# PEER gates: scattered into HBM by indirect DMAs and multiplied in by VectorE, in place of one-hot products on TensorE; a denser top-k; whole sparse rows

## The chip, the cores and the metric

The kernel runs on one core of a Trainium2 chip. The metric is the time of one execution on the device in microseconds. In this text PE is TensorE, PEld its weight loads, DVE is VectorE, ACT is ScalarE, POOL is GpSimd and SP is SyncE, as in the profile.

## What is computed

One decoder layer over 256 tokens of width 2048: a hybrid mixer, a cross attention, then the PEER expert layer, which takes two thirds of the time (571 of 1912 us lie ahead of it, with its queries) and is all that the change touches (besides sixteen stores that the front issues). For every token 8 heads pick 16 of 128 x 128 experts each:

```python
s1, i1 = lax.top_k(s[:, :, 0], 16)
s2, i2 = lax.top_k(s[:, :, 1], 16)
cand_s = s1[..., :, None] + s2[..., None, :]          # 16 x 16 sums
top_s, top_pos = lax.top_k(cand_s, 16)
experts = (i1 * 128 + i2) at top_pos
gates = softmax(top_s)
act = gelu(u[experts] @ x)                            # u, v: 16384 x 2048
y = sum over the 128 picks of gates * act * v[experts]
```

## The kernel before

*Dense and sparse tokens.* The first 224 tokens (TD) are computed densely: PE multiplies all 16384 rows of u with them, the result is multiplied by a gate that is zero for experts not picked, and PE multiplies that with all of v. The last 32 tokens (TS) are computed sparsely, by gathering the picked rows of u and v from HBM.

*Pieces and chunks.* All weights come as pieces of 128 x 1024 floats (512 KB), loaded by SP into 4 buffers (raw). ACT rounds a piece into its high part (whi, `high` and `high_v`), the rest is the low part (wlo), and PE does 16 matmuls a piece: 8 of the high part with 448 columns (inputs' high and low), 8 of the low part with 224 columns. whi and wlo have 3 buffers each, so the high part of piece n can only be made when PE has done with piece n-3. The front (mixer, cross attention, queries) has 180 pieces, the U part 256 and the V part 256. Two pieces of U are a chunk: 128 experts (one i1, all i2) for 224 tokens. Loops have 12 pieces (BODY), 6 chunks.

*Low parts.* POOL makes them for the front, all of U and the first 8 pieces of V (L438); from there on DVE makes them (`v_step`, L1437), with the low part of the gated activations (L1439).

*U.* PE leaves a chunk's sums in one of 3 PSUM banks, DVE joins their two halves (`join`, L1234), ACT applies gelu. Until chunk 48 (C_TABLES) DVE also does the top-k (L1278 to L1335): 8 pairs of lists, with a join between its parts, at fixed places of the code. The chosen i1, i2 and gates are then transposed on PE (L1925), the sparse tokens' are selected with a product (L1930). From chunk 54 (C_GATE) on, each pair of tokens gets its 128 x 128 matrix of gates: DVE writes one-hot rows of i1 and of i2 times gate (`hot_i1` L1382, `hot_i2` L1376), PE multiplies them (`gate_products`, L1899, 2 matmuls of 256 columns, 5 pairs in 6 pieces, 112 pairs), DVE adds the halves (L1405) and multiplies them into W for these tokens over all chunks (L1412). Gelus of late chunks stand in PSUM until DVE multiplies them in (`take_chunk`, L1391).

*V.* PE waits for the low part of the piece and of the gated activations (`v_ready`). Beside it, POOL issues 256 indirect gathers of 128 rows of 512 floats (four partitions share a row, 12 buffers); DVE takes each with one instruction (`u_row` L1445, `v_row` L1458). Two products (FOLD) add sums across partitions.

The order on each engine's queue is written out by hand. DVE's queue in V is: low part, low part of the gated activation, then what stands at that piece (rows, residual additions, sums of blocks). ACT's is: high part, high part of the gated activation, then its DMAs. Where an engine waits for a semaphore, all behind it in its queue waits.

## Time and profile before

| | |
|---|---|
| time, median of 3 runs | 1914.01 us (1913.36 to 1915.1) |
| span of the profiled execution | 1912.2 us |
| PE busy / PEld busy | 1896.7 us (99%) / 1758.9 us (92%) |
| DVE / ACT / POOL busy | 1383.4 us (72%) / 950.5 us (50%) / 1390.8 us (73%) |
| mean granted PE clock | 0.997 |
| HBM read and written | 443.04 MB and 4.19 MB, 234 GB/s over the span |
| front, U, V and tail (starts of their first products) | 0 to 571.3, to 1251.3, to 1899, to 1912.2 us |

In order of time:

```profile
PE   9999999999999999999999999999999999999997
DVE  7534684045545777968888888479889889999986
POOL 3867768887998999998888888976555525666711
```

A digit is the busy share of one of 40 equal slices (47.8 us), in tenths. POOL is full while it makes low parts (up to slice 26), DVE fuller in V, where it makes them.

### The profile page before, as it was taken

How to read it: one execution, taken by the hardware profiler on the slowest of the kernel's cores; microseconds unless marked ns; L12 is line 12 of the kernel's file. 1: busy time of each engine (PE TensorE's matmuls, PEld its weight loads, DVE VectorE, ACT ScalarE, POOL GpSimd, SP SyncE). 2: the span in 40 equal slices, each digit the busy share in tenths (PEclk: the TensorE clock that was granted, in tenths of full speed). 3: DMA queues.
4: the chain of work that ended last, by engine and by line, in shares of the span. 5: the costliest groups of instructions: out<-in, count | busy, mean ns of one | idle time of the engine just before them, and what ended most of it. 6: DMA issues, size and time to landing. Idle time of an engine off the chain costs nothing.

```text
span 1912.2 us, 35061 instructions
## 1 busy us (share of the span) xinstructions
PE 1896.7 (99%) x11798; PEld 1758.9 (92%) x11798; DVE 1383.4 (72%) x2585; ACT 950.5 (50%) x1342; POOL 1390.8 (73%) x708
## 2 busy tenths in 40 slices
PE   9999999999999999999999999999999999999997
PEld 7888889888999999999999999999999999999997
DVE  7534684045545777968888888479889889999986
ACT  6453355475544444544444444455555555555555
POOL 3867768887998999998888888976555525666711
PEclk9999999999999999999999999999999999999999
DMA  8544546564655666666666566689999988999984
GB/s 307 186 143 153 199 144 224 193 190 155 218 188 177 207 209 208 210 202 196 194 192 196 189 195 195 200 280 351 333 336 334 333 297 298 337 325 334 328 273 145
DMA packets 128380, 448.29 MB, mean 234 GB/s; under 512 B 16528, under 2 KB 19472, under 8 KB 127632
## 3 DMA queue, kind: packets, MB, share of 16 engines
q1 hardware_dynamic: 102240, 367.29, 58.5%
q0 software_dynamic: 20480, 67.13, 10.0%
q10 hardware_dynamic: 5584, 12.88, 2.0%
q8 instruction: 45, 0.74, 0.2%
q14 instruction: 31, 0.25, 0.0%
HBM read 443.04 MB, written 4.19 MB: 234 GB/s over the span
## 4 chain that ended last, share of the span: by engine, by line
PE 72%; POOL 17%; issue 8%; DMA 1%; DVE 1%; ACT 0%; POOLq 0%; SPq 0%; DVEq 0%; ACTq 0%
PE ps L1885 22%; PE ps L1982 22%; POOL wlo L438 17%; PE ps L1888 12%; PE ps L1985 11%; PE ps L1899 1%; PE ps L1585 1%; PE ps L1587 1%; PE ps L1586 1%; PE ps L1961 1%; DMA raw<-in_w_front 0%; PE ps L1869 0%; DMA big<-in_x_t 0%; PE ps L1963 0%; ACT whi L539 0%
## 5 line engine op out<-in xcount | busy, mean ns | idle before, releaser
L438 POOL TENSOR_TENSOR wlo<-raw,whi 128x1024 fp32r<-128x1024 f32 x436 | 1057.6, 2430 | 207.9 <-ACT whi L539 193.1
L539 ACT ACTIVATE whi<-raw 128x1024 fp32r<-128x1024 f32 x435 | 461.2, 1060 | 633.7 <-PE ps L1888 361.8
L1885 PE MATMUL ps<-x_parts,whi 128*128 128x448 f32 x2048 | 588.9, 369 | 0.0
L1982 PE MATMUL ps<-gate_parts,whi 128*128 128x448 f32 x1992 | 573.6, 369 | 0.0
L734 ACT ACTIVATE whi<-raw 128x1024 fp32r<-128x1024 f32 x256 | 271.7, 1061 | 294.9 <-PE ps L1985 255.8
L1888 PEld LDWEIGHTS ps<-x_parts,wlo 128*128 128x128 f32 x2048 | 384.7, 188 | 31.3
L1985 PEld LDWEIGHTS ps<-gate_parts,wlo 128*128 128x128 f32 x1992 | 374.2, 188 | 30.8
L1888 PE MATMUL ps<-x_parts,wlo 128*128 128x224 f32 x2048 | 386.9, 270 | 0.0
L1985 PE MATMUL ps<-gate_parts,wlo 128*128 128x224 f32 x1992 | 376.0, 270 | 0.0
L1437 DVE TENSOR_TENSOR wlo<-raw,whi 128x1024 fp32r<-128x1024 f32 x248 | 303.9, 1225 | 68.1 <-ACT whi L734 52.1
L1885 PEld LDWEIGHTS ps<-x_parts,whi 128*128 128x128 f32 x2048 | 310.3, 191 | 0.0
L1982 PEld LDWEIGHTS ps<-gate_parts,whi 128*128 128x128 f32 x1992 | 301.2, 191 | 0.1
L1585 PE MATMUL ps<-whi,x_parts 128*128 128x512 f32 (+1 forms) x544 | 214.1, 394 | 2.3 <-DVE wlo L888 2.3
L1587 PE MATMUL ps<-whi,x_parts 128*128 128x512 f32 (+1 forms) x544 | 210.1, 386 | 0.0
L1586 PE MATMUL ps<-wlo,x_parts 128*128 128x512 f32 (+1 forms) x544 | 209.4, 385 | 0.0
L465 POOL DMA_INDIRECT gather_low<-in_w_v,big x88 | 115.9, 1317 | 110.7 <-DVE big L1458 80.3
L465 POOL DMA_INDIRECT gather_low<-in_u_rows,big x88 | 103.9, 1180 | 67.3 <-DVE big L1445 54.3
L1234 DVE TENSOR_REDUCE big<-ps 128x224 f32<-128x448 f32 x128 | 79.4, 620 | 88.2 <-PE ps L1888 87.7
L1585 PEld LDWEIGHTS ps<-whi,x_parts 128*128 128x128 f32 x544 | 102.5, 188 | 23.8 <-DVE x_parts L868 3.5
L1587 PEld LDWEIGHTS ps<-whi,x_parts 128*128 128x128 f32 x544 | 102.6, 189 | 21.7
L1586 PEld LDWEIGHTS ps<-wlo,x_parts 128*128 128x128 f32 x544 | 102.7, 189 | 20.2
L1439 DVE TENSOR_TENSOR gate_parts<-big,gate_parts 128x224 fp32r<-128x224 f32 x256 | 112.7, 441 | 1.1 <-ACT gate_parts L737 0.6
(266 smaller groups left out, 2217.2 us busy)
## 6 DMA issues: line engine op xcount, KB each, us to landing
raw<-in_w_u SPq DMA_DIRECT2D x256, 512.0 KB
raw<-in_w_v SPq DMA_DIRECT2D x256, 512.0 KB
raw<-in_w_front SPq DMA_DIRECT2D x180, 512.0 KB
big<-in_mem ACTq DMA_DIRECT2D x8, 256.0 KB, 5.6
big<-in_mem_t ACTq DMA_DIRECT2D x2, 1024.0 KB, 6.2
big<-in_x ACTq DMA_DIRECT2D x2, 1024.0 KB, 7.3
x_back<-x2t_scratch ACTq DMA_DIRECT2D x2, 896.0 KB
big<-in_x_t SPq DMA_DIRECT2D x3, 512.0 KB, 8.4
```

The costliest lines, as they stand in the source:

```text
L438: nc.gpsimd.tensor_tensor(wlo[:, j % SPL, :], raw[:, j % RAW, :], whi[:, j % SPL, :], ALU.subtract).then_inc(lo_done, 1)
L465: nc.gpsimd.indirect_dma_start(ROW[at_row], None, table, bass.IndirectOffsetOnAxis(index.bitcast(I32), 0)).then_inc(row_in[at_row], 16)
L539: nc.scalar.activation(whi[:, j % SPL, :], raw[:, j % RAW, :], ACT.Copy).then_inc(hi_done, 1)
L734: nc.scalar.activation(whi[:, (V0 + j) % SPL, :], raw[:, j % RAW, :], ACT.Copy).then_inc(hi_done, 1)
L1437: nc.vector.tensor_tensor(wlo[:, s, :], raw[:, j % RAW, :], whi[:, s, :], ALU.subtract).then_inc(lo_v_done, 1)
L1585: nc.tensor.matmul(out_ap, sh, mh, start=start, stop=False)
L1586: nc.tensor.matmul(out_ap, sh, ml, start=False, stop=False)
L1587: return nc.tensor.matmul(out_ap, sl, mh, start=False, stop=stop)
L1885: nc.tensor.matmul(sums[:, 0:2 * TD], whi[:, s, cols], x_parts[:, :, m, 0:TD], start=m == 0, stop=False, skip_group_check=True)
L1888: ins = nc.tensor.matmul(sums[:, TD:2 * TD], wlo[:, s, cols], xh[:, m, 0:TD], start=False, stop=m == DC - 1, skip_group_check=True)
L1982: nc.tensor.matmul(sums[:, 0:2 * TD], whi[:, s, cols], gate_parts[:, g, :, 0:TD], start=False, stop=False, skip_group_check=True)
L1985: ins = nc.tensor.matmul(sums[:, TD:2 * TD], wlo[:, s, cols], gate_parts[:, g, 0, 0:TD], start=False, stop=False, skip_group_check=True)
```

## The change

1. *Gates by scatter.* While the front runs, ACT issues 16 stores of zeros (`zero_gates`, 896 KB each) that clear an array of 128 x 128 x 224 floats in HBM. After the top-k DVE computes one cell number for each pick and token; POOL issues 256 indirect DMAs (8 heads, 2 blocks of 128 and 96 tokens, 16 picks), each adding one gate per token into its cell. A head's DMAs wait for those of the head before, block by block. Then POOL loads the gates back, 4 chunks at a time (`load_gates`, 448 KB, 2 buffers, 32 loads), and DVE multiplies them into W (`scale_by_gate`, 128 x 896 columns): 24 of them beside chunks 112 to 126 of U, 8 at every second piece of V from piece 2.
2. *PE loses* the one-hot products, the transposes, the fold and the norm product. The selection for the sparse tokens is 16 small products instead of 4.
3. *Low parts.* POOL makes those of the front and of the first 72 pieces of U, but for the piece at place 10 of each 12, which DVE makes after the join of a chunk. All the rest of U and V is DVE's.
4. *Denser top-k.* It must end by chunk 36 (C_TABLES), not 48. A join is put in whenever the reckoned work since the last has reached 4.2 us (`topk_work`). The second list's values lie in PSUM.
5. *Whole sparse rows.* A partition takes a whole row of 2048 floats: 32 gathers of u and 32 of v, of 128 rows of 8 KB (1 MB), 3 buffers, in place of 128 and 128 of 256 KB. The four groups of partitions are added at the end by copies through DMAs issued by ACT and four additions on DVE (pieces 240, 241, 242 and 251).
6. PE waits for the join of a chunk, no longer for its gelu, to reuse the bank.

```diff
+C_TABLES = 36
+PER_LOAD = 4
+SCALED_FROM, SCALED_IN_U = 112, 24
+RING = 3
+ADDED_AT = (*range(240, 239 + GROUPS), 251)
+U_VECTOR = 10
+TOPK_NS = 4200
...
+            with pool.Fori(U0 // BODY, U0 // BODY + E_BODIES) as i:
+                for j in range(BODY):
+                    if j != U_VECTOR:
+                        rest_of(i * BODY, j)
+
+            pool.wait_ge(zeros_out, 16 * NK // (2 * PER_LOAD))
+            pool.wait_ge(cells_ready, 1)
+            for head in range(PH):
+                for tb in range(TB):
+                    if head:
+                        pool.wait_ge(scattered[tb], 16 * TOPK * head)
+                    tokens = min(P, PITCH - tb * P)
+                    for k in range(TOPK * head, TOPK * (head + 1)):
+                        nc.gpsimd.indirect_dma_start(gates_d, bass.IndirectOffsetOnAxis(CELLS[0:tokens, tb, k:k + 1].bitcast(I32), 0),
+                                                     TOP_GATES[0:tokens, tb, k:k + 1], None,
+                                                     compute_op=ALU.add).then_inc(scattered[tb], 16)
+            for tb in range(TB):
+                pool.wait_ge(scattered[tb], 16 * TOPK * PH)
+            def load_gates(k):
+                if k >= 2:
+                    pool.wait_ge(scaled_by_gate, k - 1)
+                pool.dma_start(gates_of[:, k % 2].rearrange("p a b -> p (a b)"),
...
+            for k in range(SCALED_IN_U + 2):
+                load_gates(k)
+            pool.wait_ge(picks, 1)
+            for n in range(RING):
+                gather(n)
+            for k in range(SCALED_IN_U + 2, LOADS):
+                load_gates(k)
+            for n in range(RING, 2 * PER):
+                gather(n)
...
             for j in range(BODY):
                 high_v(LAST_BODY * BODY, j)
                 gated_high(LAST_BODY * BODY - NK, j)
+                if j == 3:
+                    for k in range(2, GROUPS):
+                        act.wait_ge(group_added, k - 1)
+                        load_addend(k)
+                    act.wait_ge(group_added, GROUPS - 1)
+                    act.dma_start(ADDEND[GROUPS], gain_rows[1].partition_broadcast(TS)).then_inc(last_gain_s_in, 16)
...
             def join(k0, c):
+                nc.vector.reduce_sum(W[:, k0 + c, :], sums, AX).then_inc(sums_joined, 1)
+                if not isinstance(k0, int) or C_TABLES - 2 <= k0 + c < NK - 2:
+                    low_u(k0 * 2, 2 * c + 4)
+                    low_u(k0 * 2, 2 * c + 5)
+                elif k0 + c < C_TABLES and c % CHUNKS_PER_BODY == U_VECTOR // 2 - 2:
+                    low_u(k0 * 2, 2 * c + 4)
+            def topk_work(ns):
+                spent[0] += ns
+                if spent[0] >= TOPK_NS:
+                    spent[0] -= TOPK_NS
+                    join(0, next(chunk))
...
+            def scale_by_gate(k):
+                dve.wait_ge(act_taken, PER_LOAD * (k + 1))
+                dve.wait_ge(gates_in[k % 2], 16 * (k // 2 + 1))
+                some = W[:, PER_LOAD * k:PER_LOAD * (k + 1), :]
+                nc.vector.tensor_tensor(some, some, gates_of[:, k % 2, :, 0:TD], ALU.mult).then_inc(scaled_by_gate, 1)
+            def add_group(k):
+                dve.wait_ge(group_in[k], 16)
+                if k:
+                    dve.wait_ge(group_added, k)
+                nc.vector.tensor_tensor(Y_S, Y_S, ADDEND[k], ALU.add).then_inc(group_added, 1)
...
+                v_step(j)
+                if j % 2 == 0 and scaled < LOADS:
+                    scale_by_gate(scaled)
+                    scaled += 1
...
+                while done < 2 * PER and j >= taken(done):
+                    row_taken(done)
+                    done += 1
+                if j in ADDED_AT:
+                    add_group(ADDED_AT.index(j))
...
-                pe.wait_ge(lo_done, i * BODY + (U0 + j + 1))
+                pe.wait_ge(*low_of_u(i, j, late))
...
-            def gate_products(i, j):
-                for m in range(2):
-                    ins = nc.tensor.matmul(ps[:, 4 + j % 2, m * 2 * P:(m + 1) * 2 * P], hot1_row[:, m, :],
-                                           hot2_rows[:, j % 2, m].rearrange("p a b -> p (a b)"), start=True, stop=True)
-                ins.then_inc(gate_mat, 1)
```

## Rows read from the trace of the kernel before

**Rows 1.** Table of stretches; the second line names the columns, x counts instructions

```profile
core 0: us, PE busy (x) PEld busy (x) DVE busy (x) ACT busy (x) POOL busy (x), PEclk, DMA share, GB/s
650.00:700.00 50.00, 50.00 (x320) 47.56 (x319) 36.80 (x129) 23.66 (x31) 47.90 (x21) 1.00 0.65 207
...
1300.00:1400.00 100.00, 100.00 (x637) 95.12 (x636) 89.01 (x176) 53.00 (x80) 59.84 (x50) 1.00 0.96 338
```

**Rows 2.** Timeline of PE in U: start, length, instruction; sixteen rounds apart

```profile
699.83 0.38 PE L1888 MATMUL ps<-x_parts,wlo 128*128 128x224 f32 x2
...
709.91 0.38 PE L1888 MATMUL ps<-x_parts,wlo 128*128 128x224 f32 x2
```

**Rows 3.** Timeline of PE: first U product, transposes and selection, first V product

```profile
571.30 0.58 PE L1885 MATMUL ps<-x_parts,whi 128*128 128x448 f32 x2
...
820.37 0.81 PE L1925 MATMUL ps<-big 128*128 128x128 f32 x6
...
821.84 0.65 PE L1885 MATMUL ps<-x_parts,whi 128*128 128x448 f32 x2
...
1251.25 0.37 PE L1961 MATMUL ps<-gate_parts,whi 128*128 128x448 f32 x1
```

**Rows 4.** The gate products: count, shortest/median/longest ns, first and last start

```profile
L1899 PE MATMUL ps<-hot_rows,hot_row x224: 280/282/285, 854.7 to 1215.9; 128*128 128x256 f32 x112
```

**Rows 5.** DVE's groups in U: shapes, count, busy us, mean ns, idle before

```profile
L1234 DVE TENSOR_REDUCE big<-ps 128x224 f32<-128x448 f32 x52 | 32.2, 620 | 54.3 <-PE ps L1888 53.8
L1289 DVE TENSOR_TENSOR big<-big 128x256 f32<-128x256 f32 x16 | 26.5, 1696 | 0.0
...
L1330 DVE TENSOR_REDUCE big<-ps 128x128 f32<-128x2048 f32 x4 | 9.1, 2280 | 0.0
...
L1412 DVE TENSOR_TENSOR big<-ps,big 128x256 f32 x100 | 42.7, 427 | 15.5 <-DVE ps L1405 7.8 <-DVE big L1391 0.5
```

**Rows 6.** Timeline of DVE behind the last list: first and last of three

```profile
766.57 2.63 DVE L1315 CAST big<-big 128x512 f32<-128x512 uint32 x1
...
771.53 2.49 DVE L1317 TENSOR_SCALAR big<-big 128x256 uint32<-128x256 uint32 x1
```

**Rows 7.** Low parts on POOL and on DVE: shortest/median/longest ns, first and last start

```profile
L438 POOL TENSOR_TENSOR wlo<-raw,whi x436: 2342/2403/3395, 26.8 to 1266.0; 128x1024 fp32r<-128x1024 f32 x146
...
L1437 DVE TENSOR_TENSOR wlo<-raw,whi x248: 1211/1226/1262, 1268.7 to 1892.4; 128x1024 fp32r<-128x1024 f32 x124
```

**Rows 8.** The gathers: two groups of four, and one in the timeline of POOL

```profile
L465 POOL DMA_INDIRECT gather_low<-in_u_rows,big x88: 940/1142/1847, 1268.7 to 1524.7; - x88
...
L465 POOL DMA_INDIRECT x_back<-in_w_v,big x40: 944/1076/2652, 1552.9 to 1812.1; - x40
...
1272.69 0.95 POOL L465 DMA_INDIRECT gather_low<-in_u_rows,big  x1 [0.30 <-issue]
```

**Rows 9.** DMA issues: queue, count, KB each, median us from issue to landing

```profile
big<-in_sub_keys ACTq DMA_DIRECT2D x1, 1024.0 KB, 4.8
...
x2t_scratch<-big ACTq DMA_DIRECT2D x1, 448.0 KB, 2.9
...
x_scratch<-big ACTq DMA_DIRECT2D x1, 256.0 KB, 3.1
```

**Rows 10.** DMA rate in 40 slices of 1266 to 1300 us

```profile
GB/s 236 106 304 222 135 364 306 205 222 325 357 328 333 376 395 405 395 390 405 395 405 405 400 410 390 400 400 333 410 357 251 414 386 357 395 270 414 366 318 381
```

**Rows 11.** Timeline of ACT at the start of V

```profile
1261.70 1.74 ACTq L764 DMA_DIRECT2D big<-in_gain_rows  x4
...
1276.05 1.06 ACT L734 ACTIVATE whi<-raw 128x1024 fp32r<-128x1024 f32 x1 [2.95 <-remote]
```

**Rows 12.** DVE's row operations in V, 512 columns

```profile
L1445 DVE CUSTOM_DVE_ANT_0 gather_low<-gather_low,big 128x512 f32<-128x512 f32 x88 | 59.3, 686 | 0.0
```

**Rows 13.** Timeline of DVE at the end: scaling of the sparse rows, last joins

```profile
1895.95 0.75 DVE L1540 SCALAR_TENSOR_TENSOR big<-big,stats 128x512 f32<-128x512 f32 x1
1896.62 4.34 DVE L1471 TENSOR_REDUCE big<-ps 128x224 f32<-128x448 f32 x8
```

653 lines of the change are left out of this document (280 added, 373 removed).

## The prediction

> **What bounds the kernel now.** I read the table of stretches first [rows 1]: in each stretch of the expert part TensorE (PE) is busy for all of it, and its granted clock is 1.00, the 2.4 GHz level. Busy isn't yet bound, so I took the timeline of PE: sixteen rounds of 0.63 us lie between 699.83 and 709.91, four pieces of 2.52 us [rows 2], the same in the V part (637 matmuls, 39.8 pieces, in 100 us [rows 1]). GpSimd's low part takes 2.40 us of each 2.52 (47.90 of 50 us busy [rows 1], [rows 7]) and never makes PE wait here. So the U and V parts are 2 x 256 pieces x 2.52 = 1290 us in which PE is the bound; only what leaves PE's queue, or makes PE wait, moves the end. The front (571 us) is untouched but for sixteen DMA issues on ScalarE at about 0.45 us each (four take 1.74 [rows 11]), against 1.9 us of slack a piece; I cost them at nothing, 0 to 2 us.
>
> **Removed from PE.** The 224 gate products start between 854.7 and 1215.9 [rows 4]. By the code, 133 pieces and 111 pairs lie between the first pair and the last, so a pair costs (361.2 - 133 x 2.52) / 111 = 0.235 us, and 112 pairs cost 26.3 us. The whole of U agrees: 1251.25 - 571.30 = 679.95 us [rows 3], less 256 x 2.52 = 645.1, less two key products (7.2), the transposes and selections (1.47, from 820.37 to 821.84 [rows 3]) leaves 26.2. The fold and norm products give back 0.3. The selection becomes 16 small products, some 0.15 us each by that same stretch, 2.4 instead of 1.47: +0.9. PE's sum alone: 1914.0 - 26.3 - 0.3 + 0.9 = 1888.3. The profiled span is 1912.2, 1.8 below the median; I apply all differences to the median.
>
> **New waits.** Call S(n) the time when PE starts piece n and T(c) the end of chunk c (two pieces). ScalarE can make the high part of piece n only after S(n-2), and it is ready at S(n-2)+1.1; the low part is due at S(n), 5.04 later. VectorE (DVE) needs 1.23 us for it [rows 7], so DVE may be 2.6 us late before PE stops. That slack is the measure for everything below.
>
> (a) *Denser top-k.* Before, a pair of lists has four joins, 20.2 us, at 36.80 of 50 us busy [rows 1]: 14.8 us, less four joins of 0.62 and two additions of 1.70 [rows 5] is 8.9 us. With one operand in PSUM the addition should cost 0.43, as L1412 does [rows 5], so 9.8 us a pair. The change gives a pair 2.76 joins, 13.9 us of PE, against 9.8 + 1.7: it fits. The additions run from 0.77 to 2.63 us beside GpSimd, 1.70 on average. The Trainium skill, "SBUF — State Buffer", section "Who interferes with whom", says that a VectorE instruction with two SBUF inputs contends with a GpSimd one that reads SBUF; by it moving one operand to PSUM ends the wait, else the pair costs 12.3 + 1.7, still about 13.9.
> The end of top-k doesn't fit. By the code's counter join 25 comes right before the three casts and shifts, which take 7.5 us [rows 6] where they stand now and the counter reckons 2.0. Then one cast to PSUM and three operations of 2.3 us on 2048 columns: join 27 starts at T(25) + 0.5 + 0.8 + 7.5 + 0.7 + 3 x 2.3 + 0.5 = 16.9 ([rows 5, 6]; 0.5 is a join, 0.8 a copy and a subtraction), not +10.1. Its chunk is one of those whose join is followed by DVE's only low part of the body (piece 58), due at T(25)+15.1 and done at 18.6, or 19.8 if it waits for a GpSimd operation of 2.4 us. PE stops 3.5 to 4.7 us; I take 4.7. The same happens at piece 70 behind the gates and cells, 0 to 3.4 us, depending on whether each short operation waits for a 2.4 us one; I take 1. Sum +5.7 (0 to 9).
>
> (b) *Late U.* DVE does a join (0.62) and two low parts (2.45) a chunk of 5.04 us; the second must await ScalarE and ends at T+4.9. Due at T+7.6: nothing, 0 to 1. Cover: if it goes, each us costs a us.
>
> (c) *The scatters.* 256 DMAs on GpSimd's queue, from about T(33) to the first scale at chunk 112: some 158 pieces, 398 us, 1.55 us each. No row shows a scatter, let alone an adding one. The nearest is the indirect gather of as many rows: 0.94 us at the shortest and 1.85 at the longest in the u rows (2.65 in v's), median 1.14, plus 0.30 between two [rows 8]; a period of 1.24 to 2.15, mean 1.48. In V, DVE's two-input operations fill 64% of the time, in late U 49%, so I take 1.45: 371 us, 27 us early. Bounds 317 and 550 us. The 16 waits for the head before lie 16 DMAs (23 us) behind their DMA: nothing.
> What the trace can't give is the time that a DMA engine needs for a 4-byte element; no row has one. The Trainium skill, "DMA: Bandwidth & Descriptors", section "Specifications", says that transfers below 512 B make the DMA engine read, modify and write; no run here shows it, and it speaks against this change.
>
> (d) *Scaling in U.* 24 scales of 4 x 224 columns, at DVE's rate 1.09 us each, in 15 chunks: 0.62 + 2.45 + 1.75 = 4.8 of 5.04 us. Their gates come 448 KB at a time in two buffers, and a load is issued only when its buffer is scaled. 448 KB took 2.9 us and 1 MB 4.8 us to land [rows 9]; with 1.24 us for GpSimd's issue [rows 8] and 1.09 for a scale a pair takes 5.2 to 7.1 us where 6.3 are there. Taken: 1.5, bounds 0 and 12.
>
> (e) *Start of V.* GpSimd issues three whole-row gathers of 1 MB when U ends, and behind them, in the same queue, the load for scale 26. DVE wants scale 26 at piece 6, and PE waits unless it lands by 15 us into V. Until then weights need 208 GB/s (512 KB per 2.52 us), the queue must move 3.6 MB, and ScalarE's queue 1 MB of x rows and then 1 MB of gain. The stretch where V starts now shows 400 to 410 GB/s at the top [rows 10], and ScalarE already waited 2.95 us there [rows 11]. 3.6 MB at 200 GB/s is 18 us, with 1 MB beside it 23, plus 2.5 before they start less what a stopped PE frees: 19 to 24 us. Taken +8, bounds 0 and 12.
>
> (f) *Rows in V.* A row operation of 512 columns costs 0.69 [rows 12], nearly all by length; 2048 columns 2.3, one every 3.2 pieces: late by 1.4 us (2.3 + 1.6 - 2.52), under 2.6. The bytes and their rate stay (338 GB/s [rows 1]). Taken 0.5 (0 to 5).
>
> (g) *End.* DVE's third group sum stands at piece 242, but ScalarE issues its load after the high part of 243, at S(241)+1.8. With 3.1 us to land [rows 9], 2.3 for the sum and 1.6 for the two low parts piece 243 is ready at S(241)+8.8, due at +5.04: +3.8 (2 to 5). Sum and square at 251 and 252: +0.7. Behind the last piece the scaling of the sparse rows, 0.75 now, stands ahead of the joins, which PE's last products await [rows 13]: 2.3 instead, +1.5.
>
> **Sum.** 1888.3 + 5.7 + 1.5 + 8 + 0.5 + 3.8 + 0.7 + 1.5 = 1910, of which the waits are 21.7. I forecast 1909, as the casts' waits are taken near their top.
>
> **Rivals.**
> *No wait bites.* If DVE's lateness is absorbed and the loads land early, PE's sum holds, with the tail: 1890. For it: PE never stopped in U though DVE ran late at the same casts (joins had three banks then, no low part). Against it: orders written in the code (e, g) that no faster engine mends. 0.22.
> *The scatters come late.* Decides at 1.55 us a scatter, against 1.45 expected. Each 0.1 us above it holds DVE at chunk 112, and PE behind it, for 25.6 us; at 1.65 the time is 1935, at 2.15 it is 1909 + 152 = 2061. Slower than before. For it: the slow gathers reach past it, and adding is unpriced. Against: the mean, and only 96 tokens in every second one. 0.22.
> *The scatters' packets crowd out the weights.* The 16 DMA engines are 0.65 busy in U [rows 1], which leaves 0.5 us per scatter and engine for its 8 elements; above 60 ns an element, weights land late and PE slows in some 370 us: at 100 ns the engines would need 1.2 times their time, +74 us, 1983. 0.06. The skill's rule on transfers below 512 B would do this; its time is the one just given.
> *Gates don't leave PE's path,* because DVE is the bound in U instead: late U needs 3.1 of 5.04 us, so I give it none of its own.
>
> **Numbers.** Forecast 0.50. A difference within 0.2%, 3.8 us, is about what can't be told from no change, so faster ends at 1910.2 and slower starts at 1917.8. The forecast's own range of 1899 to 1920 splits into 0.27 faster, 0.21 same and 0.02 slower. With the first rival (0.22 faster) and the other two (0.28 slower): 0.49, 0.21, 0.30. The range takes in the first rival and a scatter of up to 1.65 us: 1889 to 1936, leaving out most of the long waits.
>
> **What would show it.** No rows of the gate products, and pieces of 2.52 us still. PE idle before its pieces 58 and 70 (about 4.7 and 1 us) released by DVE's low part; a gap of some 8 us at piece 7 of V with DVE waiting for the gate load; 4 us at piece 243 behind the addition of a group. The last scatter ends about 25 us before the first scale. Wrong if DVE's wait before its first scale is long (scatters), if ScalarE waits for weight loads in late U (packets), or if PE has no gaps (1890).

## The result, and the profile after

The changed kernel takes 2106.8 us (2106.7 to 2108.6, 4 runs), the kernel before 1914.6 us on the same chip (1913.4 to 1915.6, 4 runs): a ratio of 1.1006 with a 95% interval of 1.0991 to 1.1022, slower by 192 us. The forecast was 1909 us, with a range of 1889 to 1936: wrong in sign and in size. The profiled execution has a span of 2104.8 us.

The page's first two parts show where the time went: four slices of 53 us in which TensorE (PE), VectorE (DVE) and ScalarE (ACT) stand for all or most of the time, while GpSimd (POOL) is at 8 tenths in three of them.

```profile
span 2104.8 us, 32557 instructions
...
PE   9999999999999999999999200488999999999997
...
DVE  7543780256368976666666000476888888888877
ACT  7443364655444444444444000143555554555554
POOL 4767688778978788888888888411121120211201
PEclk9999999999999999999999655698999999999998
```

The waits of PE and DVE (engine, line, what was waited for: us in total, times, the longest):

```profile
PE ps L1903 <- DVE wlo L1296: 183.7, 6, 176.8
PE ps L1969 <- DVE gate_parts L1460: 10.0, 4, 5.8
PE ps L1951 <- DVE gate_parts L1460: 5.0, 2, 4.9
...
DVE big L1445 <- DMA gates_of<-gates_scratch: 196.2, 14, 178.1
```

And the groups (busy us, mean ns, idle before by releaser):

```profile
L512 POOL DMA_INDIRECT gates_scratch<-big x256 | 492.7, 1925 | 81.5 <-issue 81.5
...
L1445 DVE TENSOR_TENSOR big<-big,gates_of 128x896 f32<-128x896 f32 x32 | 34.9, 1089 | 196.3 <-DMA gates_of<-gates_scratch 196.2
```

They read as one chain. DVE waits 178.1 us for the first load of gates, at its first scale; PE waits 176.8 us for the low part queued behind that scale. The load stands behind 256 scatters of 1.925 us with 0.318 us between two, a period of 2.24 us and 574 us in all, from 762 to 1336 us. That mean is of two kinds: 161 scatters with a period of 2.5 us up to 1165 us, and 95 with one of 1.8 us after it, while PE and DVE stand. It is the prediction's rival "the scatters come late", which I gave 0.22, beyond the 2.15 us that it prices. It names 1.55 us as the point from which it decides.

### The profile page after: what moved, and what is told of

Same layout as the page of the kernel before. It is cut to its first block, busy times and chain, and to the rows that moved or that the text cites. A ratio compares the mean times of both kernels' runs of the same rounds, so it can differ in the third digit from the quotient of the medians.

```text
span 2104.8 us, 32557 instructions
## 1 busy us (share of the span) xinstructions
PE 1890.3 (90%) x11586; PEld 1746.5 (83%) x11586; DVE 1326.9 (63%) x1882; ACT 952.2 (45%) x1342; POOL 1209.1 (57%) x607
## 4 chain that ended last, share of the span: by engine, by line
POOL 46%; PE 31%; issue 14%; DMA 4%; DVE 3%; ACT 0%; POOLq 0%; DVEq 0%; ACTq 0%; SPq 0%
POOL gates_scratch L512 23%; POOL wlo L475 23%; PE ps L1969 18%; PE ps L1972 10%; DMA gates_of<-gates_scratch 2%; DMA raw<-in_w_v 1%; DVE big L1445 1%; PE ps L1603 1%; PE ps L1604 1%; PE ps L1605 1%; DVE wlo L1458 1%; PE ps L1951 1%; DVE wlo L1296 1%; ACT whi L787 0%; POOLq L474 0%
## 5 line engine op out<-in xcount | busy, mean ns | idle before, releaser
L475 POOL TENSOR_TENSOR wlo<-raw,whi 128x1024 fp32r<-128x1024 f32 x238 | 580.6, 2447 | 176.3 <-ACT whi L588 170.8
L1969 PE MATMUL ps<-gate_parts,whi 128*128 128x448 f32 x2000 | 580.3, 372 | 10.1 <-DVE gate_parts L1460 10.0
L512 POOL DMA_INDIRECT gates_scratch<-big x256 | 492.7, 1925 | 81.5 <-issue 81.5
L1458 DVE TENSOR_TENSOR wlo<-raw,whi 128x1024 fp32r<-128x1024 f32 x256 | 313.0, 1223 | 99.8 <-ACT whi L787 98.7
L1296 DVE TENSOR_TENSOR wlo<-raw,whi 128x1024 fp32r<-128x1024 f32 x190 | 231.7, 1225 | 137.7 <-ACT whi L588 137.7
L1445 DVE TENSOR_TENSOR big<-big,gates_of 128x896 f32<-128x896 f32 x32 | 34.9, 1089 | 196.3 <-DMA gates_of<-gates_scratch 196.2
L746 ACT ACTIVATE big<-big (+1 forms) x128 | 48.2, 376 | 196.7 <-DVE big L1303 196.5
L532 POOL DMA_INDIRECT gather_low<-in_v_rows,big x21 | 35.5, 1689 | 166.9 <-DVE big L1473 120.7
L1603 PEld LDWEIGHTS ps<-whi,x_parts 128*128 128x128 f32 x544 | 102.6, 189 | 23.9 <-DVE x_parts L933 3.4
```

Of the source, the lines that this page charges most:

```text
L475: nc.gpsimd.tensor_tensor(wlo[:, j % SPL, :], raw[:, j % RAW, :], whi[:, j % SPL, :], ALU.subtract).then_inc(lo_done, 1)
L512: nc.gpsimd.indirect_dma_start(gates_d, bass.IndirectOffsetOnAxis(CELLS[0:tokens, tb, k:k + 1].bitcast(I32), 0), TOP_GATES[0:tokens, tb, k ...
L1296: nc.vector.tensor_tensor(wlo[:, (U0 + n) % SPL, :], raw[:, n % RAW, :], whi[:, (U0 + n) % SPL, :], ALU.subtract).then_inc(lo_u_done, 1)
L1458: nc.vector.tensor_tensor(wlo[:, s, :], raw[:, j % RAW, :], whi[:, s, :], ALU.subtract).then_inc(lo_v_done, 1)
L1603: nc.tensor.matmul(out_ap, sh, mh, start=start, stop=False)
L1969: nc.tensor.matmul(sums[:, 0:2 * TD], whi[:, s, cols], gate_parts[:, g, :, 0:TD], start=False, stop=False, skip_group_check=True)
```

## Why a scatter takes 2.24 us

GpSimd's timeline beside DVE's low parts, and where DVE stands (start, length, instruction, idle time before it):

```profile
771.66 1.53 POOL L512 DMA_INDIRECT gates_scratch<-big  x1 [0.30 <-issue]
773.50 1.53 POOL L512 DMA_INDIRECT gates_scratch<-big  x1 [0.30 <-issue]
...
787.59 2.22 POOL L512 DMA_INDIRECT gates_scratch<-big  x1 [0.30 <-issue]
790.11 2.21 POOL L512 DMA_INDIRECT gates_scratch<-big  x1 [0.30 <-issue]
...
1177.41 1.54 POOL L512 DMA_INDIRECT gates_scratch<-big  x1 [0.30 <-issue]
1179.25 1.54 POOL L512 DMA_INDIRECT gates_scratch<-big  x1 [0.30 <-issue]
```

DVE's timeline in the middle of these:

```profile
787.16 1.23 DVE L1296 TENSOR_TENSOR wlo<-raw,whi 128x1024 fp32r<-128x1024 f32 x1 [0.35 <-ACT whi L588]
789.68 1.23 DVE L1296 TENSOR_TENSOR wlo<-raw,whi 128x1024 fp32r<-128x1024 f32 x1 [1.29 <-ACT whi L588]
```

From 769.8 to 774.5 us, where DVE has no low part, and from 1170 us on, where it stands, a scatter of 128 tokens takes 1.53 us (one of 96 takes 1.43). Beside low parts it takes 2.2, and the starts are 2.52 us apart: one scatter a piece of U. My theory from these rows: the instruction by itself is dear (1.5, not the gather's 0.94 of [rows 8]), and DVE's operation with two SBUF inputs adds 0.7. The rivals were room for descriptors, the addition's own traffic in HBM, and waits that would be there with fewer scatters too.

**Half the scatters.** The four first heads only; the gates of the others are left out.

```diff
-            for head in range(PH):
+            for head in range(PH // 2):
...
-                pool.wait_ge(scattered[tb], 16 * TOPK * PH)
+                pool.wait_ge(scattered[tb], 16 * TOPK * PH // 2)
```

> The changed kernel with 128 of its 256 scattering DMAs: only heads 0 to 3 are scattered, so the gates of heads 4 to 7 are left out of the dense tokens. Everything else, the 56 gate products included, is as in the changed kernel. Theory A (the count of scatters times their period of 2.24 us passes the 388 us that lie between the start at 762 us and the first scale at chunk 112): the last scatter is issued near 762 + 128 x 2.24 = 1049 us, 100 us before VectorE wants gates, the wait of 176.8 us at the last chunks of U goes whole, with about 2 us at the lower clock behind it, and the time is 2106.8 - 177 - 2 = about 1928 us. What then remains above the 1888 us of the sum is small: the gaps of 3.9 us (top-k), 4.9 and 7.1 (start of V), 2.5 (end) and the rest. Rival B (the scales in U are late by themselves, for the load of their gates or VectorE's work, and the scatters only add to it): a wait of tens of us stays before chunk 112 to 127, and the time is above 1950 us. Rival C (the scatters' packets in HBM are what costs, and half of them slows the weights as well): TensorE shows gaps at the casts in the stretch from 762 to 1049 us.

Measured: 1927.8 us (1925.6 to 1929.4, 4 runs), 1.0067 [1.0050, 1.0084] of before. The long wait is gone, 179 us with it, as the count demands. The scatters took 2.20 us each, with a period of 2.51. (The gate products that the expectation names are in neither kernel.) But 1928 is 40 us above PE's sum of 1888; that is the next section's matter.

**No addition in the DMA.** Of a cell that several heads pick, one gate stays and the others are left out.

```diff
-                                                     TOP_GATES[0:tokens, tb, k:k + 1], None,
-                                                     compute_op=ALU.add).then_inc(scattered[tb], 16)
+                                                     TOP_GATES[0:tokens, tb, k:k + 1], None).then_inc(scattered[tb], 16)
```

> The changed kernel with its 256 scatters writing plainly, without the addition in the DMA: of cells that several heads pick, one gate is kept and the others are left out. Theory A (a scatter's time is GpSimd's own work on its instruction and what VectorE's two-input operations beside it add): the scatters stay at 2.1 to 2.3 us beside VectorE's low parts and 1.5 us where VectorE stands, or fall both by the same amount if the addition is part of the dear instruction; with 1.14 us as for a gather of 2 KB rows the period would be 1.14 + 0.30 = 1.44 without VectorE and about 2.1 beside it. Rival B (the read and write back of the 4-byte addition in HBM fills the queue, and GpSimd waits for room in it): the time from issue to landing falls from 4.9 us to about 3, the scatters fall to about 1.2 us everywhere, the last ends near 762 + 256 x 1.5 = 1146 us, and the time falls by over 150 us, to about 1940 us.

> The kernel with plain scatters (the addition of several heads' gates in one cell is left out) once more, since its first time rests on one execution and kernels near it fall into slow issue of TensorE: 1926 to 1930 us in each execution if it is free of that, or over 2000 in some of them if it is a matter of chance from execution to execution.

Measured: 1928.0 us, and 1928.2 (1925.6 to 1931.6, 4 runs) the second time. GpSimd's timeline of the first, beside DVE's unchanged low part:

```profile
789.33 0.98 POOL L512 DMA_INDIRECT gates_scratch<-big  x1 [0.30 <-issue]
790.62 0.91 POOL L512 DMA_INDIRECT gates_scratch<-big  x1 [0.31 <-issue]
791.83 1.06 POOL L512 DMA_INDIRECT gates_scratch<-big  x1 [0.30 <-issue]
```

And DVE's in the same stretch:

```profile
790.88 1.23 DVE L1295 TENSOR_TENSOR wlo<-raw,whi 128x1024 fp32r<-128x1024 f32 x1 [0.41 <-ACT whi L587]
```

All 256 take 0.968 us in the mean, a period of 1.27, and end at 1088 us. So without the addition both terms are gone: 0.55 us of the instruction and nearly all of what the low parts added. I had taken the two for separate; the second hangs on the first. Of the two forecasts rival B's (1.2 us, last end at 1146 us, about 1940 us) came nearer than mine, so this run alone doesn't say whether GpSimd's own work or the traffic is the cost; the next two runs bear on that. The number of packets changes too. The DMA queue of GpSimd in 800 to 1080 us, in the changed kernel (112 scatters in that stretch) and then without the addition (223 scatters):

```profile
q0 software_dynamic: 14000, 0.06, 9.2%
```

```profile
q0 software_dynamic: 7137, 0.11, 1.8%
```

The columns are packets, MB and the share of the 16 DMA engines' time. That is 125 packets a scatter with the addition and 32 without. A dearer instruction goes with four times as many packets; that the packets are what GpSimd pays for isn't shown.

**DVE with one input from SBUF.** Low parts of U from piece 72 on subtract a stretch of PSUM; their true values are left out.

```diff
+                late = not isinstance(n0, int) or n0 + n >= 2 * C_TABLES
+                high = ps[:, 4:6, :].rearrange("p a b -> p (a b)") if late else whi[:, (U0 + n) % SPL, :]
-                nc.vector.tensor_tensor(wlo[:, (U0 + n) % SPL, :], raw[:, n % RAW, :], whi[:, (U0 + n) % SPL, :],
+                nc.vector.tensor_tensor(wlo[:, (U0 + n) % SPL, :], raw[:, n % RAW, :], high,
```

> The changed kernel, in which VectorE's low parts of the pieces of U from 72 on subtract a stretch of PSUM (banks 4 and 5) in place of the high part in SBUF: one input from SBUF in place of two, with the same number of elements. The true low part of these pieces is left out. All 256 scatters stay. Theory A (VectorE's operation with two SBUF inputs holds the port that GpSimd's scatter needs, so that each scatter grows from 1.5 to 2.2 us and falls in step with the pieces, one in 2.52 us): the scatters take 1.5 us throughout, their period is 1.5 + 0.3 = 1.8 us, the last ends near 762 + 256 x 1.8 = 1223 us, in place of 1336, and the time falls by 100 to 120 us, to about 1990 us; a wait of some 60 us stays at chunk 112, since 1.8 us is still over the 1.55 us that the window allows. Rival B (the scatters slow one another in their queue, and beside VectorE only by chance): mean period and wait stay, and the time is within 10 us of 2107.

Measured: 2000.1 us; scatters of 1.427, 1.492 and 1.769 us (shortest, median, longest), PE's longest wait 69.3 us. DVE's low part stayed at 1.22 us, so nothing else changed there; GpSimd's timeline, and then DVE's:

```profile
789.74 1.54 POOL L512 DMA_INDIRECT gates_scratch<-big  x1 [0.30 <-issue]
791.59 1.45 POOL L512 DMA_INDIRECT gates_scratch<-big  x1 [0.30 <-issue]
```

```profile
789.44 1.22 DVE L1298 TENSOR_TENSOR wlo<-raw,ps 128x1024 fp32r<-128x1024 f32 x1 [1.30 <-ACT whi L588]
```

Together they decide it: the 0.7 us goes when one of DVE's inputs moves to PSUM, with the same additions and packets, so neither the traffic nor the room brings it. For the 0.55 us it is shown that the addition brings it, not by what. A scatter costs 0.97 us plain, 1.49 with the addition (both means over those of 96 and of 128 tokens), and 2.2 with the addition beside a VectorE operation with two SBUF inputs. With 0.3 between two, the periods are 1.27, 1.8 and 2.5. The window allowed 1.55: only plain ones fit. The Trainium skill, "SBUF — State Buffer", section "Who interferes with whom", says that VectorE's two-input operation holds GpSimd up where GpSimd reads SBUF, and infers that descriptor generation escapes it. For plain scatters the trace agrees (0.97 us); for adding ones it doesn't: 2.2 against 1.49 us.

## Where the other 40 us went

All stands of PE above 0.25 us in the kernel with half the scatters, from 571 us on, are these and five of 0.3 to 0.6 us in 1174 to 1218 us:

```profile
728.62 1.11 PE L1903 MATMUL ps<-x_parts,whi 128*128 128x448 f32 x2 [3.89 <-DVE wlo L1296]
...
1230.40 0.65 PE L1903 MATMUL ps<-x_parts,whi 128*128 128x448 f32 x2 [1.78 <-DVE wlo L1296]
...
1245.07 0.71 PE L1951 MATMUL ps<-gate_parts,whi 128*128 128x448 f32 x1 [4.36 <-DVE gate_parts L1460]
...
1269.01 1.11 PE L1969 MATMUL ps<-gate_parts,whi 128*128 128x448 f32 x2 [6.13 <-DVE gate_parts L1460]
1278.23 0.68 PE L1969 MATMUL ps<-gate_parts,whi 128*128 128x448 f32 x2 [1.51 <-DVE gate_parts L1460]
...
1583.14 0.47 PE L1951 MATMUL ps<-gate_parts,whi 128*128 128x448 f32 x1 [1.39 <-DVE x_back L1489]
...
1877.57 0.67 PE L1969 MATMUL ps<-gate_parts,whi 128*128 128x448 f32 x2 [2.53 <-DVE gate_parts L1460]
```

They sum to 23.9 us, against 0.4 before. Each costs some 0.24 us more than the idle time shown: normally the next matmul starts 0.16 us before the record of the last one ends, and the first two behind a stand take 0.48 us in place of 0.41; for eleven more stands than before that is 2.6 us. Matmuls of 1.11 us in place of 0.65 mark the second loss, as in the table of stretches around two of these stands, and behind the two of 1.39 and 2.53 us (PE busy, granted clock, DMA share, GB/s):

```profile
1240.00:1245.00 5.00, 0.71 (x5) 0.85 0.45 147
1245.00:1250.00 5.00, 4.93 (x17) 0.50 0.93 293
...
1265.00:1270.00 5.00, 0.99 (x3) 0.74 1.01 378
1270.00:1275.00 5.00, 5.00 (x21) 0.57 1.00 408
...
1585.00:1588.00 3.00, 3.00 (x11) 0.50 0.56 197
1878.00:1881.00 3.00, 3.00 (x14) 0.57 0.77 210
```

Behind the three stands of 3.9 to 6.1 us PE works for 5 to 6 us at the half level of the clock, 2.5 to 2.8 us lost each time; behind those of 1.39 and 2.53 us it does so for some 3 us, 1.6 us lost; behind the other seven, of 0.3 to 1.8 us, not at all. Together PE works at the half level for 23.7 us between 571 and 1900 us, and before the change never. A round of four matmuls takes 1.17 us there in place of 0.63, so the clock costs 23.7 x (1 - 0.63/1.17) = 10.9 us. (The mean granted clocks, 0.990 and 0.997, would say 13.5, but they count time in which PE stands anyway.) With 23.5 + 2.6 of stands, 0.7 of tail, and -25.7 (products less folds, plus 0.9), that is +12.0; measured +14.3 in spans. The selection accounts for 1.1 more: 3.5 us of small products where I had 2.4. The rest, 1.2 us, I can't place.

Each of the places was then mended alone, on the kernel with half the scatters (so the gates of four heads are left out in all six). Each of these is a single execution, and the four of that kernel lie between 1925.6 and 1929.4 us: a gain of less than some 4 us isn't measured by the time, only by the stands.

**Loads of gates ahead of the gathers.**

```diff
-            for n in range(RING):
-                gather(n)
             for k in range(SCALED_IN_U + 2, LOADS):
                 load_gates(k)
+            for n in range(RING):
+                gather(n)
```

> The kernel with half the scatters (heads 0 to 3; the gates of heads 4 to 7 are left out) and one thing more: GpSimd issues its last six loads of gates ahead of its first three gathers of rows, not behind them. In the run with half the scatters TensorE stands 6.1 and 1.5 us at the first pieces of V behind the gate parts, and 4.4 us ahead of them, and its clock is at the half level for some 5 us behind each of the two longer waits. Theory A (the load of gates for scale 26 stands behind three gathers of 1 MB in GpSimd's queue and in the transfer, as the prediction has it): the waits of 6.1 and 1.5 us go, with 2 to 3 us of lost clock, and the time falls by 8 to 10 us, to about 1919. Rival B (VectorE itself is late at the start of V, with the scales of U still to catch up): the waits stay and the time is within 2 us of 1928; the gathers then come later, with no effect, since the first row is taken 18 pieces into V.

Measured: 1924.3 us. The stands at the start of V fell from 6.1 and 1.5 to 2.6 and 0.9, and the 4.4 ahead of it grew to 5.0: 3.6 us in the time, where 8 to 10 were expected. The edit does two things, for the first gather now starts at 1282.6 us, not at 1244.7; the kernel with half the scatters shows which counted. Its timelines of ACT and DVE at the stand of 6.13 us:

```profile
1266.34 1.06 ACT L787 ACTIVATE whi<-raw 128x1024 fp32r<-128x1024 f32 x1 [7.77 <-DMA raw<-in_w_v]
```

```profile
1267.42 1.23 DVE L1458 TENSOR_TENSOR wlo<-raw,whi 128x1024 fp32r<-128x1024 f32 x1 [7.58 <-ACT whi L787]
...
1270.36 1.09 DVE L1445 TENSOR_TENSOR big<-big,gates_of 128x896 f32<-128x896 f32 x1 [1.41 <-DMA gates_of<-gates_scratch]
```

PE stands there for the weights, which land late; DVE's wait for the gates comes after it and is 1.41 us. With the loads first ScalarE waited 13.4 us for weights in 1240 to 1300 us, against 18.2.

**Loads and gathers in turn.** Behind each of loads 27, 28 and 29 one gather:

```diff
-            for n in range(RING):
-                gather(n)
             for k in range(SCALED_IN_U + 2, LOADS):
                 load_gates(k)
+                if 1 <= k - SCALED_IN_U - 2 <= RING:
+                    gather(k - SCALED_IN_U - 3)
```

> The kernel with half the scatters (heads 0 to 3; the gates of heads 4 to 7 are left out), in which GpSimd issues loads of gates 26 and 27, then its first gather of 1 MB, load 28, the second gather, load 29, the third, and loads 30 and 31, in place of three gathers at once ahead of the six loads (1928) or behind load 31 (1924.3). With the loads first, ScalarE still waits 3.4, 4.1 and 0.8 us for the weights of V at 1258 to 1269 us. Theory A (the bytes that start at once at the border to V, three gathers, the loads of gates and the rows of the sparse tokens, hold up the weights): spread out they leave the weights their share, TensorE's wait at the pieces 7 to 10 falls below 1.5 us in all, and the time is 1920 to 1923 us. Rival B (only the place of the loads of gates counts): within 1 us of the 1924.3 of the loads first. The wait of 4.4 to 5 us ahead of the first V product stays in either.

Measured: 1926.4 us. Theory A's forecast failed: six stands of 0.6 to 3.0 us, 7.2 in all, where the loads first had 3.5. ScalarE waited 19.1 us for weights in 1240 to 1300 us: spread at the border to V, the gathers held them up as long as before.

**Scales from chunk 102 on.**

```diff
-SCALED_FROM, SCALED_IN_U = 112, 24
+SCALED_FROM, SCALED_IN_U = 102, 24
```

> The kernel with half the scatters (heads 0 to 3; the gates of heads 4 to 7 are left out), with the 24 scales of U spread over the chunks 102 to 126 in place of 112 to 126: about one a chunk in place of 1.6. Nothing else is changed. In the run with half the scatters TensorE stands 4.0 us behind low parts at 1174 to 1230 us and 4.4 us ahead of the first V product. Theory A (at 1.6 scales a chunk VectorE has 1.6 x 1.09 + 0.62 + 2 x 1.23 = 4.8 us of work in a chunk of 5.04 us, and each wait for a load of gates that lands 5 us after its issue, 0.8 to 2.3 us, goes straight onto the path): at one scale a chunk VectorE has 1.0 us a chunk to spare for the waits, the stands of 4.0 and 4.4 us fall below 2 us together, and the time falls by 6 to 9 us, to about 1920. Rival B (the wait ahead of V comes of the border itself, the low parts of V and the last sum, not of the scales): the 4.4 us stay and the time falls by 4 at most, to 1924.

Measured: 1918.5 us, 9.4 less. No stand is left between 729 and 1255 us, so those of the scaling stage and the one ahead of V came of 1.6 scales a chunk, as theory A has it. V's first stands remain, and are longer (5.5 and 4.7).

**30 scales from chunk 96 on** (`SCALED_FROM, SCALED_IN_U = 96, 30`).

> The kernel with half the scatters (heads 0 to 3; the gates of heads 4 to 7 are left out), with 30 of the 32 scales in U, spread over the chunks 96 to 126, in place of 24 over 112 to 126. With 24 scales from chunk 102 on (1918.5 us) the waits of the scaling stage were gone, but TensorE stood 5.5 and 4.7 us at the pieces 4 to 8 of V, with its clock at half behind each, behind the weights of V. Theory A (too many bytes start at the border to V: the weights, three gathers of 1 MB, the rows of the sparse tokens and eight loads of gates of 448 KB): with two scales left for V six loads fall away there, 2.7 MB of some 12 MB in the first 30 us, the stands fall from 10.2 to some 5 us or less with one fall of the clock less, and the time is 1911 to 1914 us. Rival B (the three gathers alone hold the weights up): the 5.5 and 4.7 us stay, and the time is within 2 us of 1918.5.

Measured: 1928.5 us. The scales began before the scatters had ended: a stand of 7.0 us at 1096 us, DVE having waited 9.4 for gates. At V's start 5.8 and 0.9 remained of 10.2. With six fewer loads 3.4 us less is left; that the other bytes hold the rest isn't shown. The time says nothing of it, since the early stand took it back.

**Group sums at 240, 241, 246 and 251.**

```diff
-ADDED_AT = (*range(240, 239 + GROUPS), 251)
+ADDED_AT = (240, 241, 246, 251)
...
+                if j == 8:
                     act.wait_ge(group_added, GROUPS - 1)
```

> The kernel with half the scatters (heads 0 to 3; the gates of heads 4 to 7 are left out) and the sums of the sparse groups put to pieces 240, 241, 246 and 251 of V in place of 240, 241, 242 and 251; nothing else is changed. Theory A (the third sum waits for its addend, loaded only when the first sum frees its place, and TensorE stands 2.5 us behind it, at the 243rd piece): the wait of 2.5 us goes with about 1 us of lost clock, and the time falls by 2 to 4 us, to about 1925. Rival B (the load takes as long wherever it is awaited): the wait moves to the piece 246, and the time stays at 1928.

The last two lines are in ScalarE's queue: its wait for the third sum, with the load behind it, moves five pieces back, which the expectation leaves unsaid.

Measured: 1921.8 us, 6.1 less. The stand of 2.5 us is gone, and with it the 1.6 us at the half level of the clock behind it; another 1.6 us is no merit of the edit (the fall of the clock behind 728 us was shorter by that in this execution).

**Casts counted at 7.6 us.**

```diff
-TOPK_NS = 4200
+TOPK_NS = 4400
...
-            topk_work(2000)
+            topk_work(7600)
```

> The kernel with half the scatters (heads 0 to 3; the gates of heads 4 to 7 are left out) and the three casts of the top-k counted at their own 7.6 us in place of 2.0, so that VectorE takes a chunk of U up earlier behind them; the interval between chunks is 4.4 us of counted work in place of 4.2. Theory A (the casts of 2.6, 2.5 and 2.5 us with no chunk between them delay the next sums and low part, and TensorE stands 3.9 us at 725 us, with a clock at half for about 6 us behind it): the wait falls below 1 us, the clock stays at full, and the time falls by 5 to 7 us, to about 1922. Rival B (the longer interval only moves the wait to another place in the top-k): a wait of 2 us or more elsewhere in 660 to 760 us, and no gain above 2 us.

Measured: 1926.7 us. The stand of 3.9 us is gone, and V starts 3.9 us earlier; yet the end gains 1.2. The fall of the clock isn't gone: it comes at 762 us, in the small products of the selection with no stand before it, and lasts as long (PE's table of stretches; busy, clock, DMA share, GB/s):

```profile
763.00:769.00 6.00, 6.00 (x22) 0.50 0.52 96
```

A gain of 1.2 us isn't measured, only the stand.

## Plain scatters with all mended, and a slowdown that stays open

With plain scatters (the addition left out; 1928 us) the counted casts gave 1922.0 us, and 30 scales from 102 with the group sums, at the old count, 1911.0, 0.16% under the 1914.2 of before. Each was run once.

> The kernel with plain scatters (1928.0 us; the addition of several heads' gates in one cell is left out) with one thing more: the casts of the top-k counted at 7.6 us and the interval at 4.4 us. In the kernel with all the edits (2225 us) TensorE took seven pieces of U in 300 us while the plain scatters ran, with issue gaps of 2.3 to 3.2 us between single matmuls and nothing to wait for; this run has only that edit which shifts the start of the scatters against TensorE's program. Theory A (the moment at which the row of plain scatters begins, against TensorE's change from one loop of its program to the next, decides whether its issue starves): the slow issue is here too, and the time is over 2100 us. Rival B (the edits at the scales and groups bring it, by the place of TensorE's program or otherwise): 1921 to 1928 us and no slow issue.

> The kernel of 2225 us with the old counting of the casts (2.0 us, interval 4.2 us) put back: plain scatters (the addition of several heads' gates in one cell is left out), 30 scales in U from chunk 102 on, group sums at 240, 241, 246 and 251. Theory A (the start of the scatters against TensorE's program decides): no slow issue, and the time is 1928 less 6 to 12 for scales, loads and groups: 1915 to 1922 us. Rival B (the edits at the scales and groups bring it): over 2100 us.

No slow issue in either. Both together should have given some 1905.

> The changed kernel with all 256 scatters, plainly written (the addition of several heads' gates in one cell is left out), 30 scales in U from chunk 102 on, the group sums at 240, 241, 246 and 251, and the casts of the top-k counted at 7.6 us: what the change would bring if nothing of it came late. The plain scatters end near 1087 us, ahead of chunk 102 at about 1098. Theory A (the parts add up: 1928.0 with plain scatters, 9.5 less for the earlier scales, 3 to 5 for the groups, 4 to 7 for the casts with their clock, 4 to 7 for the loads taken from the border to V): 1903 to 1908 us, the first of these kernels under the 1914 of before, by 0.3 to 0.6%. Rival B (the gain of one place is given back at the next, as in the kernel with the casts counted, where 7 us of stand and clock gave 1.2 us): 1912 to 1918 us.

Measured: 2225.1 us (2214.8 to 2228.8, 4 runs). Tables of stretches (PE, PE's weight loads, DVE, ACT, POOL busy; clock; DMA), of this kernel:

```profile
780.00:1080.00 300.00, 50.29 (x115) 32.61 (x114) 11.20 (x11) 9.55 (x12) 227.33 (x233) 0.50 0.06 13
```

And of the one with plain scatters and counted casts alone:

```profile
780.00:1080.00 300.00, 300.00 (x1906) 285.38 (x1906) 182.82 (x179) 142.86 (x179) 227.46 (x239) 1.00 0.73 208
```

While the scatters run, at the same rate in both, PE issues a sixteenth of its matmuls in the one (DVE and ACT do as little), and nothing that the profile shows is waited for (PE's timeline in the first):

```profile
856.34 0.34 PE L1906 MATMUL ps<-x_parts,wlo 128*128 128x224 f32 x1 [3.15 <-issue]
859.85 0.53 PE L1903 MATMUL ps<-x_parts,whi 128*128 128x448 f32 x1 [3.17 <-issue]
```

In this stretch both kernels give PE the same instructions, and the scatters start within 1.0 us. So neither the scatters' rate nor PE's work is the cause by itself. The slow issue goes on to 1115 us, where the last scatter ends at 1090. Shifting PE's program by four small products didn't help either:

> The kernel of 2225 us (plain scatters, the addition of several heads' gates in one cell left out, and all the other edits) with TensorE's program shifted: four small products behind the selection of the picks are made twice, with the same result, which adds 0.5 us. Up to chunk 102 the kernel of 2225 us gives TensorE the same instructions in the same order as the kernel of 1922 us (plain scatters and counted casts), and the scatters start within 1 us of each other there, so the instructions of that stretch can't be the cause. Theory A (where TensorE's program lies in memory, or the moment at which its next part is fetched, decides): the shift takes the slow issue away, and the time is 1903 to 1908 us, or changes its length by over 50 us. Rival B (it is something else in that kernel): 2215 to 2230 us as before.

Measured: 2229.3 us (2226.0 and 2232.7), the same stretch with 118 matmuls, as rival B has it. It goes with the program, not with chance: all four executions of the one kernel and both of this one are slow, and all five of the kernel with plain scatters alone are good. Nor is it the chip: chip 0 has run a slow one and a good one. The profile's instruction queues moved 4 packets in 780 to 1080 us of the slow kernel and 3 in the good one, so no stream of instruction loads shows there either. Its cause stays open.

**Merging in VectorE.** A whole kernel must add the gates of one cell. Here VectorE does it, one operation for each of 256 picks, and the scatters are plain; the loads first, the group sums at 246 and the counted casts are in it.

```diff
+    nc.vector.scalar_tensor_tensor(SAME[:, n % 4, :], EXPERT[:, tb, :], EXPERT[:, tb, k:k + 1], TOP_GATES[:, tb, :],
+                                   ALU.is_equal, ALU.mult, MERGED[:, tb, k:k + 1]).then_inc(merged, 1)
```

> A whole kernel, with nothing left out. VectorE first merges the gates: for each of the 256 picks of a token row one operation over the 128 picks of that token adds the gates of the same expert (16 of them ahead of the scatters, the rest 5 or 6 a chunk over 42 chunks of U), so that all copies of a cell carry the same sum. GpSimd scatters the merged gates plainly, without the addition in the DMA, and the three placings of the last three kernels are in it (loads of gates first, group sums at 240, 241, 246 and 251, casts counted at 7.6 us). Theory A (the addition in the DMA was the dear part, 0.97 + 0.30 us a scatter without it): scatters end near 775 + 256 x 1.28 = 1103 us, before VectorE wants gates at 1150, and the time is that of the plain scatters, 1928, less 9 for the loads, 3 for the groups and 6 for the casts, plus 0 to 8 for VectorE's 256 operations of 0.2 to 0.35 us: 1906 to 1918, about 1910 us, so 0 to 0.4% under the kernel before. Rival B (VectorE has no room for the merges: its chunk has 5.04 us, of which two low parts and a sum take 3.2): TensorE stands at low parts in 775 to 990 us, by some 0.5 us a chunk, 20 us in all, and the time is 1925 or above. Rival C (VectorE's operations with two inputs slow the plain scatters too): the scatters rise to over 1.3 us, and a wait comes back at chunk 112.

Measured: 1924.5 us (1919.4 to 1924.9, 4 runs), 1.0050 [1.0033, 1.0067] of before. It is above theory A's range. Rival C holds in part: the scatters rise to 1.16 us in the mean, up to 2.0, under its 1.3, and no long wait comes back at chunk 112. PE doesn't stand at low parts from 762 to 1170 us, so rival B doesn't hold, though its time fits. A merge starts every 0.27 us (0.36 and 0.14 us, overlapping, and not the 0.5 of the next expectation); sixteen of them, one of 2.54 us beside a low part of GpSimd, took 6.6 us, and a stand of 5.7 us followed at 761 us. Its successor read one operand from PSUM, spread the merges, had the scales from 108, and issued loads and gathers in turn:

> A whole kernel, with nothing left out: the merged gates of the last whole kernel (1924.5 us), with (1) the expert numbers that VectorE's merge compares read from PSUM, so that it has one input from SBUF; (2) only 4 merges ahead of the next chunk and 6 to 7 in each of the next 38, in place of 16 and then 5.7 in 42; (3) the 24 scales of U from chunk 108 on in place of 112; (4) gathers and loads of gates in turn at the border to V. In the last whole kernel TensorE stood 5.7 us at 761 us behind 16 merges of 0.5 us with the casts, the scatters took 1.16 us in the mean and 1.4 to 1.8 beside merges, against 0.97 without, and the border to V cost 4.7 + 2.6 + 1.1 us. Theory A (each of these is what I name): the stand at 761 us falls below 1 us (with 2 to 3 us of clock, -7), the scatters take 0.97 to 1.05 us and end near 1105 us, ahead of chunk 108 at 1130, the stands of the scaling stage and the border fall by about 5 us, and the time is 1924.5 - 7 - 5 - 1 = about 1911 us (1906 to 1916), level with the kernel before. Rival B (1.26 scales and 6.5 merges a chunk only move VectorE's delay about): within 3 us of 1924.

> The whole kernel of 2127.9 us with one operand put back: the expert numbers of VectorE's merges are read from SBUF and not from PSUM. In the run before, TensorE's own issue was slow in seven stretches of 9 to 55 us between 783 and 1181 us (matmuls 0.7, 1.4, 2.1 us apart with nothing to wait for that the profile shows), always some 12 to 20 scatters into a row that ran at 1.21 us each. Theory A (the reads of PSUM by the merges slow TensorE's issue): no such stretch, and the time is 1924.5 less 5 for the stand at 761 us, plus 10 to 20 for scatters that end near 1145 us, behind chunk 108 at 1130: 1930 to 1940 us. Rival B (rows of scatters at 1.21 us, with nothing of VectorE between them, are what slows the issue, whatever the merges read): the scatters stand beside two-input operations again and take 1.16 us in the mean, but in the stretches in which GpSimd is ahead of the merges they run at 1.21 us and TensorE's issue slows down again: over 1980 us.

Measured: 2127.9 us (2121.1 to 2136.3, 4 runs), and 2114.3 with the operand in SBUF again. Both show PE's slow issue in several stretches of 9 to 55 us during the scatters, so the operand isn't what brings it; rival B's time came true, its cause is untested. No whole kernel of these beats the one before.

## The prediction, point by point

- *Removed from PE* (26.3 us): nothing in the runs speaks against it; the accounts above close within 1.2 us with it. The selection cost 3.5 us, not 2.4.
- *(a) Top-k.* Right: one stand of 3.89 us before a low part at 728.6 us, predicted 4.7 (3.5 to 4.7) at piece 58; none for piece 70 (predicted 1). An addition with one operand in PSUM took 0.41 us in the mean, 0.43 predicted, not the 1.70 of [rows 5].
- *(b) Late U.* Right: no stand from 730 to 1160 us.
- ***(c) The scatters.* The step that failed.** I took a period of 1.45 from a gather's mean and set "Bounds 317 and 550 us". It measured 2.24 and 574 us, beyond the upper bound. Two terms were missing: the addition (+0.55 us on GpSimd) and the 0.7 us beside low parts, at one a piece (2.5 us from start to start). I had reckoned by DVE's busy share (49% against 64%), but the period locks to the pieces: what counts is that each scatter meets a low part. "adding is unpriced" stood in the text; an unpriced part of 256 equal instructions with 7% to spare should have carried more than 0.22. The rival's own rule held, as arithmetic must once the mean is known: (2.24 - 1.55) x 256 = 177 us, measured 176.8.
- *(d) Scaling in U.* 3.0 us in four stands in the changed kernel, predicted 1.5; and 4.9 us ahead of V from the same cause, not foreseen (the run with scales from 102 shows it).
- *(e) Start of V.* The size was right by luck: 5.8 and 1.3 us against 8. The cause was another: ScalarE waited 7.5 us for weights ahead of the first stand, and DVE's wait for gates (1.7 us) came behind it. Putting the loads first, and so the gathers later, took away 4.1 of 7.6 us of stands.
- *(f) Rows.* A row operation took 2.29 us (2.3 predicted). Beside the rows PE stood 0.4 us once (0.5 predicted), and 1.4 us at the middle of V where it was 0.4 before, not foreseen.
- *(g) End.* 2.5 us behind the group sum (3.8 predicted), gone when the sum moved. The tail grew by 0.7 (1.5 predicted).
- *Packets crowd out the weights.* Refuted: in the changed kernel PE has no stand from 770 to 1160 us, at an adding scatter every 2.5 us. Its 14000 packets took 9.2% of 16 engines in 280 us, 29 ns each, where the rival needed 60. In the plain kernel there is none either, at a scatter every 1.27 us.
- *The clock.* No term of the sum had it. It cost 10.9 us with half the scatters, more than any single stand.

Without late scatters the forecast of 1909 would still have been 19 us short: 11 of it the clock.

## What to carry to other kernels

Price an instruction that will run hundreds of times from its own form; a DMA that adds isn't a DMA that copies, and beside a VectorE operation with two SBUF inputs it grew again. Compare its period with the window it must fit, and when that is within some tens of per cent, treat "late" as the likeliest case until the form has been timed. When TensorE has been without gaps, charge new stands with a lower clock as well: here 2.5 to 2.8 us behind each stand of 3.9 to 6.1 us, 1.6 us behind two of 1.4 and 2.5, and nothing behind seven others. Removing a stand needn't remove the fall; once it came 34 us later, in a row of small products.

## What the runs showed of the chip that I had not expected

- An indirect scatter of 128 4-byte elements: 0.96 us plain, 1.54 adding, 2.2 adding beside VectorE with two SBUF inputs (for 96 elements 0.91, 1.43 and 2.2). Its packets: 32 plain, some 125 adding, 29 ns each.
- A gather of 128 rows of 8 KB takes GpSimd 1.67 us at the median, against 1.14 for rows of 2 KB [rows 8].
- Plain scatters in an unbroken row can go with an issue rate of TensorE that is sixteen times lower (115 matmuls in 300 us, against 1906), in some programs and not in others. What decides it isn't known.
